# A seventh product in the last quarters: grouping the first two down chunks of the final MLP quarter and turning three chunks in the last block

## What is computed

```python
x = x + diff_attention(rms_norm(x, a_norm_g), a_w_qkv, ...)        # layer 0
x = x + square(relu(rms_norm(x) @ w_up[0])) @ w_down[0]            # 2048 -> 8192 -> 2048
k_nope, k_rope, v = shared_latent_kv(rms_norm(x), w_dkv, ...)
x = x + mla_attention(rms_norm(x), w_dq, w_uq, ..., k_nope, k_rope, v)   # layer 1
x = x + square(relu(rms_norm(x) @ w_up[1])) @ w_down[1]
return rms_norm(x, final_norm_g)
```

## Time and profile before

| what | us |
|---|---|
| median of three runs | 1983.12 |
| the profiled execution | 1983.5 |
| its span, first to last instruction | 1981.7 |
| TensorE busy | 1971.5 (99%) |
| VectorE busy | 1620.7 (82%) |
| ScalarE busy | 1208.8 (61%) |
| GpSimd busy | 34.3 (2%) |

### The profile page before, as it was taken

How to read it: one execution, slowest core, us unless ns; L and a number is a source line. 1 busy time by engine, 2 the same in 40 slices (tenths; PEclk the granted TensorE clock), 3 DMA queues, 4 the chain that set the end, 5 groups by cost and what they waited for, 6 DMA issues and landing times.

```text
span 1981.7 us, 24530 instructions
## 1 busy us (share of the span) xinstructions
PE 1971.5 (99%) x9092; PEld 1644.3 (83%) x9092; DVE 1620.7 (82%) x1979; ACT 1208.8 (61%) x1547; POOL 34.3 (2%) x45
## 2 busy tenths in 40 slices
PE   9999999999999999999999999999999999999998
PEld 7888888888888888888888998888888888888886
DVE  7789996678988998898866787667998898898865
ACT  6555555557667566656646665556566666665653
POOL 0000000000000000000000000000000000000000
PEclk9999999999999999999999999999999999999999
DMA  8655556766787587677766554677587677658673
GB/s 296 223 170 181 180 169 202 225 198 215 225 243 232 190 244 231 219 233 222 244 213 192 146 152 145 227 225 224 188 233 239 225 225 235 217 201 255 219 233 107
DMA packets 269407, 418.24 MB, mean 211 GB/s; under 512 B 18801, under 2 KB 88817, under 8 KB 269297
## 3 DMA queue, kind: packets, MB, share of 16 engines
q1 hardware_dynamic: 251920, 395.82, 61.6%
q0 software_dynamic: 3456, 12.58, 3.4%
q10 hardware_dynamic: 13920, 8.39, 1.5%
HBM read 379.00 MB, written 2.10 MB: 192 GB/s over the span
## 4 chain that ended last, share of the span: by engine, by line
PE 96%; issue 2%; DVE 1%; ACT 0%; POOL 0%; POOLq 0%; DVEq 0%; ACTq 0%
PE acc L608 23%; PE acc L610 23%; PE acc L609 23%; PE side L843 3%; PE side L844 3%; PE side L842 3%; PE acc L842 2%; PE acc L844 2%; PE acc L843 2%; PE acc L628 2%; PE acc L629 2%; PE acc L630 2%; PE acc L961 1%; PE acc L962 1%; PE acc L963 1%
## 5 line engine op out<-in xcount | busy, mean ns | idle before, releaser
L1733 DVE TENSOR_TENSOR wlo<-raw,whi 128x1024 fp32r<-128x1024 f32 x572 | 679.9, 1205 | 168.6 <-ACT whi L1108 166.9
L1108 ACT ACTIVATE whi<-raw 128x1024 fp32r<-128x1024 f32 x572 | 586.8, 1045 | 347.6 <-PE acc L610 281.0
L608 PE MATMUL acc<-whi,opA 128*128 128x512 f32 (+2 forms) x1072 | 414.6, 387 | 0.0
L610 PE MATMUL acc<-whi,opA 128*128 128x512 f32 (+2 forms) x1072 | 413.9, 386 | 0.0
L609 PE MATMUL acc<-wlo,opA 128*128 128x512 f32 (+2 forms) x1072 | 413.8, 386 | 0.0
L608 PE MATMUL acc<-whi,opB 128*128 128x512 f32 x1008 | 393.5, 390 | 0.1
L610 PE MATMUL acc<-whi,opB 128*128 128x512 f32 x1008 | 392.4, 389 | 0.0
L609 PE MATMUL acc<-wlo,opB 128*128 128x512 f32 x1008 | 392.2, 389 | 0.0
L610 PEld LDWEIGHTS acc<-whi,opA 128*128 128x128 f32 x1072 | 201.3, 188 | 40.2
L608 PEld LDWEIGHTS acc<-whi,opA 128*128 128x128 f32 x1072 | 201.3, 188 | 40.0
L609 PEld LDWEIGHTS acc<-wlo,opA 128*128 128x128 f32 x1072 | 201.3, 188 | 39.8
(11 more groups left out here) (380 smaller groups left out, 2644.1 us busy)
## 6 DMA issues: line engine op xcount, KB each, us to landing
raw<-in_w_up SPq DMA_DIRECT2D x128, 1024.0 KB, 5.9
raw<-in_w_down SPq DMA_DIRECT2D x128, 1024.0 KB, 5.1
raw<-in_a_w_qkv SPq DMA_DIRECT2D x44, 1024.0 KB, 5.2
raw<-in_a_w_o SPq DMA_DIRECT2D x16, 1024.0 KB, 5.1
prob<-o_sb SPq DMA_DIRECT2D x128, 128.0 KB, 2.6
raw<-in_b_w_o SPq DMA_DIRECT2D x16, 1024.0 KB, 5.2
raw<-in_w_ukv SPq DMA_DIRECT2D x32, 256.0 KB, 4.0
prob<-o_sb ACTq DMA_DIRECT2D x48, 128.0 KB, 4.4
```

The lines of the kernel that those rows point to most:

```text
L608: mm(o, a_hi, w_hi, start=start, stop=False)
L610: done = mm(o, a_lo, w_hi, start=False, stop=last and c == chunks - 1)
L1108: done = fn(whi[:, place:place + ch, 0:n], raw[:, r, c0:c0 + ch, 0:n], ACT.Copy)
L1733: done = tt_(wlo[:, place:place + ch, 0:n], raw[:, r, c0:c0 + ch, 0:n], whi[:, place:place + ch, 0:n].bitcast(F32), ALU.subtract)
```

## The change

In the last quarter of both layers `first_down` is now used as in the others: a group of seven in place of quads (0, 2) and (1, 2), with one more set of activation forms (`FORM_SETS`). Its shares are combined by VectorE after half 3 of block j = 2, scaled by ScalarE after half 5 and added by GpSimd. Since chunks 0 and 1 are complete only then, what uses them moves back: in layer 0 chunk 0 is turned after half 9 of block 2 (second half of block 3) and chunks 1 and 2 after halves 3 and 6 of block 3, with their moves and copies; in layer 1 the squares of chunks 0 and 1 and their products with the final gains stand after half 9 of block 2. The load of the final gains' second part is issued a little later.

```diff
 DOWN_FIRST = ((0, 0), (0, 1), (1, 0), (1, 1))
 DOWN_LAST = ((0, 3), (1, 3))
-LAST_DOWN = ((0, 0), (0, 1), (0, 2), (1, 0), (0, 3), (1, 1), (1, 2), (1, 3))
...
-    return made
+    return made + [("first", l, QUARTERS - 1)]
...
-FORM_SETS = 1 + 2 * (QUARTERS - 1)
+FORM_SETS = 2 + 2 * (QUARTERS - 1)
...
-                    if j == JB - 1 and q < QUARTERS - 1:
+                    if j == JB - 1:
                         sp.wait_ge(form_step, 4 * (FORM_SETS * l + 2 * q + 1) + 4)
...
-                    order = DOWN_FIRST + ((0, 2), (1, 2)) + DOWN_LAST
-                    if q == QUARTERS - 1:
-                        order = LAST_DOWN
-                    for k, (j, r) in enumerate(order):
+                    for k, (j, r) in enumerate(DOWN_FIRST + ((0, 2), (1, 2)) + DOWN_LAST):
...
-                first_down(QUARTERS - 1)
-                with sp.Fori(2, JB) as j:
-                    down(QUARTERS - 1, j)
+                q = QUARTERS - 1
+                first_down(q)
+                for j in range(2, JB):
+                    for r in range(4):
+                        src = W_DOWN[l][:, KC * q + 4 * r:KC * q + 4 * r + 4, NB * j:NB * j + NB]
+                        quad(B_MLP[l] + 2 * JB * q + JB + j, r, src, later=int(j == 2 and r == 0))
...
+                shared_sums_added(l, ("first", l, QUARTERS - 1), 0)
...
-                    if q == QUARTERS - 1:
-                        for k, (j, r) in enumerate(LAST_DOWN):
-                            plain_quad(k, j, r)
-                        return
...
-                        if hf == 5:
+                        if hf == 5 and q < QUARTERS - 1:
                             down_forms(q, 1)
...
-                def last_chain(q):
-
-                    return {3: lambda: square_second(q, 1), 4: lambda: hid_high(q, JB - 2),
-                            7: lambda: hid_high(q, JB - 1)}
...
                 q = QUARTERS - 1
-                for j in range(JB):
-                    s = (j + 1) % 2
-                    asides = {} if j else last_chain(q)
-                    if l == 1 and j == 0:
-                        asides[9] = last_gains
-                    if j == 1:
-                        asides[6] = lambda: x_squares(squares_from, 1, u[1] + U_QUARTER * q + U_UP + 1)
-                    if v_out is not None and j:
-                        asides[7 if j == 1 else 4] = lambda: x_move(v_out + j - 1)
-                        asides[10 if j == 1 else 7] = lambda: x_hi(v_out + j - 1, None)
+                first_down(q)
+
+                def first_squares():
+                    act.wait_ge(shared_added, 32 * DOWN_SHARE["first", l, q] + 32)
+                    for j in range(2):
+                        s = (j + 1) % 2
+                        x_squares(squares_from + j, s, u[s] + U_QUARTER * q + U_UP + 1)
+
+                def last_share():
+                    scale_shared(("first", l, q))
+
+                for j in range(2, JB):
+                    b, s = B_MLP[l] + 2 * JB * q + JB + j, (j + 1) % 2
+                    asides = {}
+                    if v_out is not None and j == 2:
+                        asides = {5: last_share, 10: lambda: x_move(v_out)}
+                    elif v_out is not None:
+                        asides = {4: lambda: x_hi(v_out, None), 5: lambda: x_move(v_out + 1), 7: lambda: x_hi(v_out + 1, None), 8: lambda: x_move(v_out + 2), 10: lambda: x_hi(v_out + 2, None)}
+                    elif j == 2:
+                        asides = {4: last_gains, 5: last_share}
+                    if j == 2:
+                        asides[9] = first_squares
                     if l == 1 and j == JB - 1:
                         for hf in range(3, 8):
-                            split(B_MLP[l] + 2 * JB * q + JB + j, hf)
+                            split(b, hf)
                     else:
-                        body(B_MLP[l] + 2 * JB * q + JB + j, asides, nxt=nxt if j == JB - 1 else None)
-                    if j and (l == 0 or j < JB - 1):
+                        body(b, asides, nxt=nxt if j == JB - 1 else None)
                         x_squares(squares_from + j, s, u[s] + U_QUARTER * q + U_UP + j // 2 + 1)
...
                     split(b + 1, 4)
-                    form_sums(sqT, down_set(q, 1))
+                    if q < QUARTERS - 1:
+                        form_sums(sqT, down_set(q, 1))
                     split(b + 1, 5)
                     split(b + 1, 6)
-                    form_low(down_form(1), down_set(q, 1))
+                    if q < QUARTERS - 1:
+                        form_low(down_form(1), down_set(q, 1))
...
-                def add_first(q):
-
-                    dve.wait_ge(shared_added, 32 * DOWN_SHARE["first", l, q - 1] + 32)
-                    dve.wait_ge(pe_halves, 8 * (B_MLP[l] + 2 * JB * q + JB) + 10)
-                    add_scaled(None, 1, 2 * (u[1] + U_QUARTER * q + U_UP), slice(0, NB))
...
-                sum_second(QUARTERS - 1, 1)
                 q = QUARTERS - 1
-                for j in range(JB):
+                sum_second(q, 1)
+                first_down(q)
+
+                def turned(j):
+                    s = (j + 1) % 2
+                    dve.wait_ge(shared_added, 32 * DOWN_SHARE["first", l, q] + 32)
+                    x_turn(v_out + j, s, 2 * (u[s] + U_QUARTER * q + U_UP + j // 2 + 1))
+
+                def weighted():
+                    with_norm_weight(0)
+                    with_norm_weight(1)
+
+                for j in range(2, JB):
                     b, s = B_MLP[l] + 2 * JB * q + JB + j, (j + 1) % 2
-                    added = 2 * (u[1 - s] + U_QUARTER * q + U_UP + (j - 1) // 2 + 1)
-                    asides = {} if j else last_chain(q)
-
-                    def first_added():
-                        add_first(q)
-                        if v_out is not None:
-                            x_turn(v_out, 1, added)
-
-                    if j == 1:
-                        asides = {5: first_added}
-                        if v_out is not None:
-                            asides[10] = lambda: x_lo(v_out, None)
-                    elif v_out is not None and j:
-                        asides = {7: lambda: x_lo(v_out + j - 1, None)}
-                    if l == 1 and j:
-                        asides[8 if j == 1 else 4] = lambda: with_norm_weight(j - 1)
+                    asides = {}
+                    if j == 2:
+                        asides = {3: lambda: combine(SHARE["first", l, q], down_shared),
+                                  9: weighted if l else lambda: turned(0)}
+                    elif l == 0:
+                        asides = {3: lambda: turned(1), 4: lambda: x_lo(v_out, None), 6: lambda: turned(2), 7: lambda: x_lo(v_out + 1, None), 10: lambda: x_lo(v_out + 2, None)}
                     if l == 1 and j == JB - 1:
                         for hf in range(3, 8):
                             split(b, hf)
-                            if hf in asides:
-                                asides[hf]()
+                            if hf == 4:
+                                with_norm_weight(j - 1)
                         continue
                     body(b, asides, nxt=nxt if j == JB - 1 else None)
-                    if j == 0:
-                        continue
                     add_scaled(b, s, 2 * (u[s] + U_QUARTER * q + U_UP + j // 2), slice(NB * j, NB * j + NB))
-                    if v_out is not None:
-                        x_turn(v_out + j, s, 2 * (u[s] + U_QUARTER * q + U_UP + j // 2 + 1))
+                    if v_out is not None and j == JB - 1:
+                        turned(j)
```

More of the change, by code:

```diff
@@ L2367, in up_pair @@
                         split(b + 2, hf)
-                def last_chain(q):
-                    return {3: lambda: up_turn(q, JB - 1), 4: lambda: hid_low(q, JB - 2), 7: lambda: hid_low(q, JB - 1)}
                 body(B_MLP[l], {7: lambda: x_lo(v_in + JB - 1, G_MLP[l]), 8: lambda: stream_stats(2 * l + 1, True),
```

## The result

The changed kernel takes 1990.45 us in the median of 8 runs (1988.64 to 1992.3), the kernel before 1983.17 in the same sessions (1982.58 to 1985.15, 8 runs): ratio 1.0035, 95% interval 1.0026 to 1.0045. So it is 7.3 us slower, where 8.6 were forecast (1991.7 us in the range 1984 to 1999).

What follows compares the result with a forecast made beforehand. TensorE, busy 99% of the span, was taken to bound the kernel. Matmuls saved -2.3, layer 0's turning +10.9, layer 1 0: +8.6 us on 1983.5 gives 1992.1, as median 1991.7 us; range 1984 to 1999.

Steps and rivals of the forecast that it cites:

- adding landed: Layer 0, last quarter: GpSimd's second adding transfer lands 13.4 us after scaling starts, at 20.0; range 9.8 to 15.1.
- half 22 late by: Layer 0, block DKV: first weight half of chunk 3, wanted at 59.8 us, comes 10.9 us late.
- Seven for eight: Last quarter of each layer: 48 plain matmuls become 42 in a group, saving 1.14 us each, 2.28 us in both.
- The turning decides: Layer 0's last block and DKV: turning, moving and copying chunks one at a time is the deciding term, 10.9 us lost.
- The size of the turning: Layer 0: late turning of the chunks loses 10.9 us, with ends of 2.0 and 18.6 us.
- the estimate of 1989.7 us: Total time if the adding lands 6.5 us after scaling began, by the skill's fit; layer 0's loss then 8.9 us.
- A load beside the move: Layer 0: a chunk's move takes 4.7 us without a weight load, 8.0 us taken with one beside it.
- Layer 1 at 0: Layer 1's last block: squares and final-gain products wait for the adding without loss; taken at 0, range 0 to 0.9 us.
- The chain fits: Rival, layer 0: weight loads draw back, moves land in 4.7 us; time 1982.8 or 1984.8 us; chance 0.20.
- The clock falls: Rival: TensorE drops to 1.2 GHz after gaps of 3.7 and 4.3 us, costing some 2 us; 1993.7 us; chance 0.08.
- the signs of being wrong: No layer 0 waits, several us waited in layer 1, a wait in the last quarter's group, or clock below full after gaps.
- The size of the gaps: TensorE's stops in layer 0's last block and DKV: 3.7 and 4.3 us, then a 1.4 us wait.

Runs made afterwards that it cites:

- the mended kernel: Changed kernel plus a second pair of buffers, layer 0's steps reordered and layer 1's squares and final-gain products placed later: 1980.63 us, ratio 0.9989.
- layer 0 alone: Changed kernel with the group of seven and late turning only in layer 0, layer 1 as before the change: 1988.87 us.

## Why the prediction was right

The forecast's chain, counted from the start of block j = 2 (1014.5 us in the changed kernel), against the trace:

| step | forecast | measured |
|---|---|---|
| adding landed | 20.0 | 18.5 |
| move 0 landed | 27.6 | 26.8 |
| split 12 ready (wanted 32.6) | 32.3 | 30.7 |
| move 1 landed | 41.5 | 39.6 |
| split 15 late by | 4.0 | 2.1 |
| move 2 landed | 53.9 | 49.4 |
| split 19 late by | 9.4 | 5.9 |
| move 3 landed | 68.3 | 65.1 |
| half 22 late by | 10.9 | 7.8 |

- **Seven for eight**, -2.3 us: right; 12 matmuls fewer, the new groups without a wait, and the mended kernel measures 2.4 under before.
- **The turning decides**: right, and shown from three sides: without the group the loss is the same, with two pairs of buffers in a fitting order it is gone, with short moves its waits fall to 2.1 us by the view.
- **The size of the turning** came out 3.1 us too large. 2.0 of that is the start of move 0, taken at 22.9 us and measured at 20.9. The adding was taken at 13.4 us from the scaling to the landing and measured at 11.9, at 1033.1 us, some 0.2 before VectorE came to the turning behind its split (1033.32); so it held nothing, as the kernel without groups shows. The Trainium skill's fit (DMA: Bandwidth & Descriptors, "Anatomy of one DMA — SWDGE (gpsimd) path") gives 6.5 us as an estimate and was further off. But any landing that early leaves the turning where it is, and so the estimate of 1989.7 us that goes with it lies 0.75 us from the measured time and my own number 1.25. The moves were taken at 4.7, 8.0, 8.0 and 8.0 and took 5.9, 7.6, 5.3 and 8.9: 1.0 less in all, move 2 being the one far off. For move 0 I had said that no load falls due; one was issued at 1033.43, 2.0 us ahead of it, and its transfers took 3.0 to 3.9 us. 0.1 lies in the other steps.
- **A load beside the move**: right as the cause; 4.7 us without one was forecast, 4.6 measured. What I had not seen is that the order within the overlap matters: with a load issued 1.2 us ahead of the move (1057.42) all four transfers landed by 5.3 us; with one issued among them (1047.52, 1072.00) the last ones took 5.6 to 6.9 us each. My 8.0 for all three overlooked that.
- **Layer 1 at 0**: wrong. It cost 1.4 us. The adding took 15.8 us from the scaling, just beyond the 15.1 I had as the longest. The three cases of the earlier trace rows already held a second transfer issued late (872.45, 4.97 us of "issue"); I took the spread as chance, where it recurs by the transfer. Layer 0 got a quick pair, layer 1 a late one.
- **The chain fits**: its condition was right: with three moves at 4.6 us the time is 1984.85 us, and the rival's was 1982.8 to 1984.8. The moves did not meet it by themselves.
- **The clock falls**: it did, but only behind the first gap, 2.1 us where I had expected one of 3.7; behind the later gaps it stayed full. I had named this among the signs of being wrong. Behind the first gap the next wait hides it, as argued, and layer 0 alone loses as much with the clock full. Why it falls stays open; it is not tied to the length alone: 2.3 us in layer 0 alone left the clock full, 1.9 us with two buffers did not.
- **The size of the gaps**: being late by 4.0, 9.4 and 10.9 us means gaps of 4.0, 5.4 and 1.5 us, and not the 3.7, 4.3 and 1.4 that stand beside them in the forecast. The forecast's sum does not rest on these. Measured were 2.1, 1.7 and 1.8, and 0.2 with the slow stretch between the first two.

The errors lie on opposite sides (3.1 us too much in layer 0, 1.4 too little in layer 1), and so the time came out nearer than the terms did; that part is luck.

## What to carry to other kernels

Where a saving makes its user work later, price the chain behind the user, step by step, against what the bounding engine wants next: here 2.3 us of matmuls were bought with 7 to 8 us of waits in a stage that had been slack. If one pair of buffers carries a loop of copy, transfer and copy back, a second pair and an order in which no finished step stands behind an unfinished one can give back all of it; and holding a large load that is not urgent until a small urgent transfer has landed was the cheapest mending here (two waits, 5.6 us).

## What the runs showed of the hardware

- Four transfers of 128 KB issued 0.65 us apart by ScalarE landed in 2.6 to 2.7 us each with the weight load held back; the last of a move, with a 1 MB load issued from 0.9 us ahead of it to 0.4 us behind it, landed after 5.6 to 7.2 us (kernels before and after).
- Issuing the four took ScalarE 2.7 us, and its next work began only behind them (1051.12 to 1053.88 us with two buffers).
- GpSimd's second adding transfer of 512 KB (the large transfers) is issued late, behind 3.8 to 6.9 us of "issue", where it is number 4, 8, 10, 16, 22 or 28 of the run, right after the first of the pair has landed (1952.3 and 1952.57 us), in every kernel here that has so many.
- The granted clock fell to about 0.6 for 4 to 5 us behind two gaps of 2.1 and 1.9 us and stayed full behind others of 1.4 to 2.3 us. What tells these cases apart stays open.
